# The sample's pieces moved forward among the units of prompt attention

## What is computed

```python
o_c, o_s = _cmp_slc_attend(q, pos, *keys)          # compressed blocks, then the 16 best blocks of 64 keys
o_w = _attend(q, kwb, vwb, _win_mask(pos, kpos))   # the window of 512 keys
o_nsa = _gate_merge(gates, o_c, o_s, o_w)          # three gates per head
```

## Time and profile before

| | us |
|---|---|
| median of 3 runs | 2892.95 (2892.53 to 2897.22) |
| profiled execution | 2892.73 |
| its span | 2891.2 |
| TensorE busy | 2678.3 (93%) |
| VectorE busy | 1047.4 (36%) |
| ScalarE busy | 764.5 (26%) |
| GpSimd busy | 343.9 (12%) |

### The profile page before, as it was taken

The page is one execution under the profiler, slowest core; times in us unless marked ns, Lnnn a source line. Parts: engine busy times, 40 slices in busy tenths (PEclk is TensorE's granted clock), DMA queues, the critical chain, the costliest instruction groups (busy, mean ns, idle before and its releaser), DMA issues.

```text
span 2891.2 us, 49314 instructions
## 1 busy us (share of the span) xinstructions
PE 2678.3 (93%) x17788; PEld 2394.8 (83%) x17788; DVE 1047.4 (36%) x2036; ACT 764.5 (26%) x1167; POOL 343.9 (12%) x321
## 2 busy tenths in 40 slices
PE   7999999998888899999899999999988998999996
PEld 7999788896456889999899997888844567999996
DVE  2222121535654632231432211223456547222415
ACT  2222000421442332231232210013214423222313
POOL 0000000024221200013100000001241311000240
PEclk9999999997996899999999999999969959999998
DMA  3222543114421122222122234421153301222222
GB/s 132 87 87 87 155 137 110 57 61 133 140 76 58 59 73 87 87 83 81 70 88 87 87 114 146 132 84 61 53 176 100 89 30 59 88 87 87 89 80 80
DMA packets 110002, 265.81 MB, mean 92 GB/s; under 512 B 15347, under 2 KB 85138, under 8 KB 90770
## 3 DMA queue, kind: packets, MB, share of 16 engines
q1 hardware_dynamic: 99778, 233.21, 23.9%
q0 software_dynamic: 10080, 30.73, 3.4%
HBM read 258.15 MB, written 14.24 MB: 94 GB/s over the span
## 4 chain that ended last, share of the span: by engine, by line
PE 50%; issue 36%; DVE 3%; POOL 3%; DMA 2%; SPq 2%; ACT 1%; DVEq 1%; POOLq 1%; PEldq 0%; PEld 0%; ACTq 0%
PE PS L463 49%; POOL wo_lo L394 2%; SPq L320 1%; POOL wi_lo L452 1%; DVEq L1429 1%; DMA WO<-wo_dram 1%; POOLq L403 1%; DMA M<-slc_k_dram 1%; PE PS L953 0%; DVE sm L1893 0%; DVE xs L1547 0%; DMA WI<-wi_dram 0%; POOLq L407 0%; DVE wi_lo L1432 0%; ACT WO L1118 0%
## 5 line engine op out<-in xcount | busy, mean ns | idle before, releaser
L463 PE MATMUL PS<-xs,wi_hi 128*128 128x272 f32 x5376 | 1020.1, 289 | 20.1 <-DVE wi_lo L1432 18.2
L463 PE MATMUL PS<-xs,wi_lo 128*128 128x272 f32 x3088 | 899.9, 291 | 0.0
L463 PEld LDWEIGHTS PS<-xs,wi_hi 128*128 128x128 f32 x5376 | 850.5, 190 | 21.4 <-issue 21.4
L463 PEld LDWEIGHTS PS<-xs,wi_lo 128*128 128x128 f32 x3088 | 590.7, 191 | 0.0
L394 POOL TENSOR_TENSOR wo_lo<-WO,wo_hi 128x2816 fp32r<-128x2816 f32 x24 | 150.8, 6282 | 1914.0 <-ACT wo_hi L1118 1914.0
L463 PE MATMUL PS<-H,WO 128*128 128x272 f32 x1408 | 332.5, 398 | 6.8 <-DMA WO<-wo_dram 5.3
L1432 DVE TENSOR_TENSOR wi_lo<-WI,wi_hi 128x2048 fp32r<-128x2048 f32 x85 | 194.8, 2292 | 370.0 <-ACT wi_hi L1118 370.0
L463 PEld LDWEIGHTS PS<-H,WO 128*128 128x128 f32 x1408 | 269.3, 192 | 68.0 <-issue 12.5
L463 PE MATMUL PS<-wo_hi,xs 128*128 128x352 f32 x960 | 239.0, 328 | 14.5 <-DVE xs L1547 8.2
L1118 ACT ACTIVATE wi_hi<-WI 128x2048 fp32r<-128x2048 f32 x85 | 162.8, 1915 | 290.3 <-DMA WI<-wi_dram 290.3
L463 PE MATMUL PS<-h_hi,wo_hi 128*128 128x272 f32 x704 | 207.4, 295 | 24.5 <-POOL wo_lo L394 14.1
(11 more groups left out here) (202 smaller groups left out, 3045.3 us busy)
## 6 DMA issues: line engine op xcount, KB each, us to landing
WI<-wi_dram SPq DMA_DIRECT2D x100, 1024.0 KB, 4.9
WO<-wo_dram SPq DMA_DIRECT2D x44, 1408.0 KB, 6.0
M<-cmp_t_dram SPq DMA_DIRECT2D x256, 128.0 KB, 2.3
M<-slc_k_dram SPq DMA_DIRECT2D x128, 64.0 KB, 2.1
M<-slc_k_dram POOLq DMA_DIRECT2D x128, 64.0 KB, 2.4
M<-slc_v_dram SPq DMA_DIRECT2D x128, 64.0 KB, 2.1
M<-slc_v_dram POOLq DMA_DIRECT2D x128, 64.0 KB, 2.3
o_win_s_dram<-win_rows_dram POOLq DMA_DIRECT2D x2, 4064.0 KB, 4.1
```

The costliest lines, as they stand in the source:

```text
L463: return nc.tensor.matmul(out, lhsT, rhs, start=start, stop=stop, skip_group_check=True)
```

## The change

The table of steps is changed, and nothing else. keys_1 to cmp_columns and the compressed branch up to rank stay. keys_2 goes from step 4 to 3, keys_3 from 10 to 8, spread_selection from 13 to 12, mask from 14 to 13. All pieces behind the mask, from win_scores to take_outputs, come three steps earlier.

```diff
 AT = dict(keys_1=0, cmp_scores=1, cmp_softmax=2, cmp_weights=4, cmp_turn=5, cmp_columns=6, cmp_outputs=7, cmp_take=8,
-          importance=9, rank_ties=10, rank=11, spread_selection=13, mask=14, keys_2=4, keys_3=10, win_scores=17,
-          win_rows=18, win_exp=19, win_turn=21, win_columns=22, win_values=26, win_take=27, slc_rows_0=20, slc_exp_0=21,
-          slc_rows_1=22, slc_exp_1=23, slc_turn_0=27, slc_values_0=34, slc_values_1=39, slc_turn_1=41,
-          slc_values_2=48, slc_values_3=55, slc_take=56, turn_outputs=58, take_outputs=59)
+          importance=9, rank_ties=10, rank=11, spread_selection=12, mask=13, keys_2=3, keys_3=8, win_scores=14,
+          win_rows=15, win_exp=16, win_turn=18, win_columns=19, win_values=23, win_take=24, slc_rows_0=17, slc_exp_0=18,
+          slc_rows_1=19, slc_exp_1=20, slc_turn_0=24, slc_values_0=31, slc_values_1=36, slc_turn_1=38,
+          slc_values_2=45, slc_values_3=52, slc_take=53, turn_outputs=55, take_outputs=56)
```

## The result

The changed kernel takes 2917.97 us (median of 6 executions, 2910.83 to 2925.02) against 2896.78 us of the kernel before in the same sets of runs: a ratio of 1.0069, 95% interval 1.0051 to 1.0088. It is slower, by about 20 us (0.69%). A second set of runs gave 2919.55 us and 1.0070 (1.0055 to 1.0085). The forecast was 2905.3 in a range of 2893 to 2915: the sign was right, the size fell short, and the time lies above the range.

The account below looks back on a forecast made before the run. TensorE was taken to set the pace except where pieces hold it up in the attention stretches. Terms 5.2 + 1.6 + 2.2 + 2.8 + 0.8 = 12.6 us on 2892.7 gave 2905.3 us, range 2893 to 2915.

Parts of the forecast that it names:

- What bounds the kernel: TensorE sets the pace, 93% busy, except at three places: keys_2's page wait, units 10 to 12's ranking, units 18 to 24.
- The wait for pages, 6.4 and 8.5 us: At keys_2, pages start no sooner, so TensorE's waits grow from 2.12 (layer 0) and 4.27 us (layer 1).
- Key group 2, 5.2 + 1.6 us: keys_2 from unit 4 to 3: 2.6 us per layer of uncovered work, plus 1.6 for layer 0's piece at low clock.
- product(1): Probabilities-times-values step of unit pair 1, behind unit 6's scores; its 0.91 us wait for ScalarE was expected to go.
- Key group 3, 2.2 us: keys_3 from unit 10 to 8: no longer hidden behind VectorE's ranking, 1.1 us per layer slower; bounds 0 and 2.2.
- Units 14 to 25, 2.8 us: Window and mask pieces three units earlier: 1.4 us per layer slower, dips left unchanged; bounds -2.3 to +3.3 per layer.
- Units 25 to 63, 0.8 us: Value pieces moved between odd and even units cover waits differently: 0.4 us per layer slower; bounds -1.7 to +1.5.
- The base: The profiled execution's 2892.7 us, to which the forecast added its terms, uncorrected because the runs' median was 2892.95.
- One more dip everywhere: Rival: a third dip in each middle stretch (3.8 us) and a longer one in layer 0 (1.5): 2910.6 us; chance 0.18.
- The clock pays it back: Rival: dips of units 14 to 25 go, slc_values_3 and layer 0's keys_2 at full clock: 2892.1 us, no change; chance 0.20.
- The pages did not land sooner: Denies the rival that key pages land sooner while VectorE stands, 2.2 us less, 2903.1 us; chance 0.04.
- The bound of a measurement, 0.2%: Whole kernel: about 0.2%, 5.8 us, was taken as what a measurement can tell from no change.

Follow-up runs that it names:

- e3_keys2_only: Against the kernel before, only key group 2 moved, from unit 4 to 3; ratio 1.0008 (0.9996 to 1.0021).
- e12_before_again: The kernel before itself, unchanged, one more traced execution; 2901.5 us.
- e2_keys_only: Against the kernel before, only key groups 2 (unit 4 to 3) and 3 (unit 10 to 8) moved; ratio 1.0030 (1.0019 to 1.0042).
- e4_pieces_only: The changed kernel with key groups 2 and 3 back at units 4 and 10; ratio to the kernel before 1.0027 (1.0010 to 1.0043).
- e9_keys_late: Against the kernel before, key group 2 moved later to unit 6 and key group 3 to unit 11; ratio 0.9998 (0.9982 to 1.0013).
- e18_before_filled_again: The kernel before with unread products ahead of the turns of units 17, 18, 20, 21 and 22, second set; ratio 1.0020 (0.9999 to 1.0041).
- e8_pieces_by_2: Against the kernel before, pieces behind the mask two units earlier, spread_selection and mask one, key groups unmoved; ratio 1.0017 (1.0003 to 1.0030).

## Why the prediction was right and wrong

In short: what failed is the step that left the low-clock dips of units 14 to 25 as they were. The waits had been summed rightly; with the same sum in another order the low clock there went from 13.7 to 30 us a layer.

- **What bounds the kernel**: right. But for 3.4 us, which the rest of the program took less in this pair of executions, the difference lies in the attention stages, most of it at the three places named.
- **The wait for pages, 6.4 and 8.5 us**: right in sum (14.9 against 15.4). The start at 738.4 us in layer 0 was wrong by 3.6 us (734.8), because the stage itself began 3.5 us sooner; measured from unit 0's maximum it is the 15.4 us of before. I had tied the pages to the start of the span, and named a sooner start as a sign of being wrong, which it is not: the stage's start moves from execution to execution. For layer 1 the 2163.5 us could not hold either, since my own terms put that stage later.
- **Key group 2, 5.2 + 1.6 us**: e3_keys2_only measured 2.3 (-1.2 to +6.1). The 0.91 us that I gave back for product(1) came: unit 6 took 3.6 us instead of 4.6. The 1.6 us for a unit's scores and turn should have been 1.8, the step from 2153.16 to 2154.94 in the trace of before. What failed is that I took layer 0's form from one execution. In the other form, e12_before_again's, the pages have landed and the move costs nothing there. Where the wait is there, the low clock behind it is longer than priced: in the profiled execution units 3 to 7 grew by 6.2 and 5.7 us, 11.9 together, where my two terms make 6.8 and 8.3 with the upper bound. The low level lasted 13.7 and 17.1 us there, before 0 and 3.4.
- **Key group 3, 2.2 us**: mis-sized; the traces give 5.2 (2.3 and 2.9 a layer), the medians 6.4. My bound was 2.2 a layer. Unit 8 itself took 2.2 us longer, as expected (5.6 us, before 3.4); what I set against it did not come back. Taking its 1.9 us out of the ranking's shadow leaves TensorE idle there (3.9 to 5.0 us in units 7 to 14 of e2_keys_only, before 2.4) and a low stretch behind it (clock 0.92 in layer 1). That the two terms for the key groups sum to the measured 8.7 is luck: one was too high by what the other was too low.
- **Units 14 to 25, 2.8 us**: this is the step that failed. The waits, replayed from the row durations, were right, even better than I believed: I expected 1.4 us more idle time a layer and found 8.6 against 8.6. I expected over 3 us ahead of the product of unit 22; the wait is 4.0 us one step sooner, ahead of the turn in step 21, and 1.2 us at the product. Then I wrote "I leave the dips as they are". They were what changed. Of the 12.7 us that units 14 to 25 grew by, 3.7 are, by my count, the work that moved in from behind, and the other 9.0 are the same work at half the clock. The traces agree as far as they can be read: TensorE is busy at the low level for 28.5 us, before 9.6, and half of the difference is 9.5. The bound of +3.3 a layer counted one more dip like the two; it had to count that a stretch of 20.5 us can stand where one of 6.8 stood, and that the end of another, 3 us, reaches in from before unit 14. Why the order of the waits has this effect stays open: these runs show that it has, not by what rule.
- **Units 25 to 63, 0.8 us**: the term came out at its lower bound. 5.6 us less, of which 3.7 moved out by the same count, leaves -1.9 a layer; my -1.7 was the case that slc_values_3 escapes the low clock of the earlier trace rows, and it did: it takes 1.96 us at 2339.84.
- Together the pieces cost 12.7 - 5.6 = 7.1 us a layer in the profiled execution, against 1.8 forecast; by the medians, in e4_pieces_only, 7.8 us in all against 3.6.
- **The base**: I added 12.6 us to 2892.7, which was a short execution. The kernel before has a median of 2896.8 beside the changed kernel, and 2898 to 2899 in the larger sets. So 4 of the 12.7 us by which the forecast missed are the base; the other 8 to 9 are the difference, 12.6 forecast and 20 to 21 measured.
- **The rivals.** "One more dip everywhere" named the mechanism and priced it at 5.3 us; it had 0.18. "The clock pays it back" (0.20) was the same mechanism with the other sign; it did not come. e9_keys_late shows its mirror, where the clock takes back what the waits gave. The pages did not land sooner for any standstill of VectorE: with a wait of 9.2 us they came 18.3 us behind unit 0's maximum in layer 1, before 17.6.
- **The bound of a measurement, 0.2%**, was too fine. Single executions of the kernel before lay between 2886.6 and 2910.6 us in these sets, and with 6 to 12 executions the intervals are 0.2 to 0.5% wide in all.

## What to carry to other kernels

When a reordering leaves the sum of TensorE's idle time as it was, ask still how the idle time is spread: here 8.6 us of waits went with 13.7 us of low clock in one order and with 30 us in another. Price a move at full clock, then add a term for the low stretches with bounds of several such stretches on both sides, and let no gain or loss of a few microseconds stand on one trace. Where the waits can't be removed, short products that nobody reads are a cheap experiment and sometimes a gain: with the key groups late they made the best version, 0.995 to 0.996 of the kernel before, and in the order of the kernel before they made it no faster (1.0026 and 1.0020).

## What the runs showed of the hardware

- The low clock is not a fixed price for a wait. In the kernel before a wait of 4.27 us for pages is followed by a low stretch of 3.4 us; in e18_before_filled_again one of 4.68 us, at the same instruction, by 13.7 us (units 3 to 7 at a clock of 0.71 against 0.92). The waits in front are the same to 0.4 us.
- The same program gets different clocks in its two layers (e8_pieces_by_2: 0.76 and 0.85) and in two executions. Ahead of layer 0's stage the low clock lasted 37.5 us in one trace of the kernel before (and 6.8 us more after a return) and 64.9 us in one piece in the other, which shifts the stage by 9 us. Where the pages have landed meanwhile, units 3 to 7 give some of it back: 2.1 us in the kernel before (16.5 and 14.4), 10.2 us in the changed one (22.7 and 12.5). Units 14 to 25 can then take it again: 45.4 us in e12_before_again's layer 0, at a clock of 0.77, where the other trace has 43.0 at 0.84. Much of the spread from execution to execution seems to be of this kind: across the executions of e9_keys_late the time rises from 2889.5 to 2911.0 us as the mean clock falls from 0.935 to 0.928.
- The Trainium skill, page TensorE: Matmul & The Clock Gate, Part 1, says that one kernel can show a different number of products at the low clock from run to run, since what watches TensorE's activity is not in step with the program, and puts the warm-up's price at under 1% of a typical kernel. The traces above agree that it varies; here a fraction of a percent was the whole verdict.
